# Where the tiles of a two-block transformer kernel start within the 2048-byte rows of SBUF

## The reference, cut to what matters

```python
def swiglu(h, w_gu, w_down):
    g, u = jnp.split(h @ w_gu, 2, axis=-1)          # 1024 -> 2 x 2816
    return (jax.nn.silu(g) * u) @ w_down            # 2816 -> 1024
...
for l in range(DEPTH):                              # first block, DEPTH = 2
    x = x + FFN_RESIDUAL * (1 + mod[2])[:, None, :] * swiglu(h, ffn1_w_gu[l], ffn1_w_down[l])
    x = x + (1 + mod[5])[:, None, :] * hybrid_mixer(...)
    x = x + FFN_RESIDUAL * (1 + mod[8])[:, None, :] * swiglu(h, ffn2_w_gu[l], ffn2_w_down[l])
...
for i in range(DEPTH):                              # second block
    x = x + g1[:, None, :] * mixed                  # even_mixer or odd_mixer
    x = x + g2[:, None, :] * conv_ffn(h, ffn_w_in[i], ffn_conv_w[i], ffn_conv_b[i], ffn_w_out[i])
```

## Time and profile before

| | |
|---|---|
| median of three runs | 3612.19 us |
| the profiled execution's own time | 3611.59 us |
| its span | 3609.8 us |
| PE busy | 3360.8 us, 93% |
| DVE, ACT, POOL busy | 54%, 33%, 28% |
| DMA | 116 GB/s on average |
| mean granted clock of TensorE | 0.952 of full speed |

### The profile page before, as it was taken

How to read it: one execution, slowest core, us unless ns; L and a number is a source line. 1 busy time by engine, 2 the same in 40 slices (tenths; PEclk the granted TensorE clock), 3 DMA queues, 4 the chain that set the end, 5 groups by cost and what they waited for, 6 DMA issues and landing times.

```text
span 3609.8 us, 41457 instructions
## 1 busy us (share of the span) xinstructions
PE 3360.8 (93%) x14717; PEld 2649.8 (73%) x14717; DVE 1946.7 (54%) x2809; ACT 1194.0 (33%) x1790; POOL 1011.5 (28%) x713
## 2 busy tenths in 40 slices
PE   6999979999999999978999998999999988599998
PEld 4888756678878888755688886756788867478886
DVE  6534575565356533666665334346654379864443
ACT  3222233532223222323432223254333243243332
POOL 2815530056184800181064004700730021000000
PEclk7999999999999999989999998979999999799999
DMA  6635552155364633352155334601543333023332
GB/s 206 198 109 153 151 156 66 30 163 168 103 190 132 198 95 95 97 174 66 41 175 150 93 94 146 186 1 53 174 140 96 92 97 84 12 70 99 97 94 83
DMA packets 577054, 417.65 MB, mean 116 GB/s; under 512 B 29979, under 2 KB 537226, under 8 KB 575798
## 3 DMA queue, kind: packets, MB, share of 16 engines
q1 hardware_dynamic: 532434, 283.99, 26.8%
q0 software_dynamic: 34304, 121.64, 11.3%
q10 hardware_dynamic: 10212, 10.68, 1.0%
HBM read 408.89 MB, written 6.06 MB: 115 GB/s over the span
## 4 chain that ended last, share of the span: by engine, by line
PE 78%; DVE 15%; ACT 3%; issue 2%; ACTq 0%; DMA 0%; DVEq 0%; SPq 0%
PE bank L313 23%; PE bank L314 23%; PE bank L315 23%; PE bank L1213 2%; PE bank L1244 2%; DVE w_lo L290 1%; DVE tmp L427 1%; PE bank L545 1%; PE bank L1234 1%; DVE w_lo L299 1%; DVE h_lo L437 1%; DVE s_x L2280 1%; DVE s_t L2271 1%; DVE folded L487 1%; DVE s_x L2277 1%
## 5 line engine op out<-in xcount | busy, mean ns | idle before, releaser
L313 PE MATMUL bank<-h_hi,w_hi 128*128 128x512 f32 x2656 | 1055.5, 397 | 74.9 <-DVE w_lo L290 35.9
L314 PE MATMUL bank<-h_lo,w_hi 128*128 128x512 f32 x2656 | 1047.0, 394 | 0.0
L315 PE MATMUL bank<-h_hi,w_lo 128*128 128x512 f32 x2656 | 1045.7, 394 | 0.0
L299 DVE TENSOR_TENSOR w_lo<-raw,w_hi 128x1024 fp32r<-128x1024 f32 x438 | 624.4, 1426 | 594.6 <-ACT w_hi L282 593.7
L282 ACT ACTIVATE w_hi<-raw 128x1024 fp32r<-128x1024 f32 x438 | 461.8, 1054 | 718.7 <-PE bank L315 718.6
L313 PEld LDWEIGHTS bank<-h_hi,w_hi 128*128 128x128 f32 x2656 | 505.7, 190 | 200.5 <-issue 48.9
L315 PEld LDWEIGHTS bank<-h_hi,w_lo 128*128 128x128 f32 x2656 | 505.3, 190 | 109.0
L314 PEld LDWEIGHTS bank<-h_lo,w_hi 128*128 128x128 f32 x2656 | 505.9, 190 | 105.5 <-issue 0.2
L624 POOL TENSOR_TENSOR mod_acc<-mod_acc,mod_w 128x1024 f32<-128x1024 f32 x168 | 473.1, 2816 | 14.0
L313 PE MATMUL bank<-hid_hi,w_hi 128*128 128x512 f32 x1056 | 421.5, 399 | 13.9 <-DVE w_lo L299 13.6
L314 PE MATMUL bank<-hid_lo,w_hi 128*128 128x512 f32 x1056 | 419.2, 397 | 0.0
(11 more groups left out here) (314 smaller groups left out, 3465.6 us busy)
## 6 DMA issues: line engine op xcount, KB each, us to landing
raw<-in_ffn_w_gu SPq DMA_DIRECT2D x176, 512.0 KB, 3.8
mod_w<-in_w_ada POOLq DMA_DIRECT2D x128, 512.0 KB, 4.1
mod_w<-in_mod_w POOLq DMA_DIRECT2D x96, 512.0 KB, 4.2
raw<-in_ffn_w_in SPq DMA_DIRECT2D x88, 512.0 KB, 3.8
raw<-in_ffn_w_down SPq DMA_DIRECT2D x64, 512.0 KB, 4.1
raw<-in_w_in SPq DMA_DIRECT2D x34, 512.0 KB, 4.0
raw<-in_ffn_w_out SPq DMA_DIRECT2D x32, 512.0 KB, 4.1
raw<-in_ffn_w_down SPq DMA_DIRECT2D x32, 384.0 KB, 3.5
```

Of the source, the lines that this page charges most:

```text
L299: loop(nc.vector.tensor_tensor(w_lo[:, u % 2, :], raw[:, u % 2, :], w_hi[:, u % 2, :].bitcast(F32), ALU.subtract), "split_lo", times)
L313: nc.tensor.matmul(dst, a_hi, b_hi, start=start, stop=False)
L314: nc.tensor.matmul(dst, a_hi, b_lo, start=False, stop=False)
L315: return nc.tensor.matmul(dst, a_lo, b_hi, start=False, stop=stop)
```

## The change

Four things are done to the placement, and nothing else. The small tiles that are not streamed in 512 columns (`cols`, `ident`, `ones`, `cact`, `stat`, `eps`, `misc`, `shape_col`, `inv_rms`, `folded_col`) come first, from byte 16512 on. The cursor is then rounded up to the next multiple of 2048, 22528, and the tiles from `x` to `sq` follow. `group` becomes 129024, which is 63 x 2048. Four tiles (`folded`, `swap`, `coef`, `smx`) go to a strip above the last multiple of 2048 in the usable bytes. No instruction is added, removed or reordered.

```diff
+ROW = 4 * S
...
+        top = nc.sbuf_usable_end // ROW * ROW
+        tail = [top]
...
-            assert where[0] <= nc.sbuf_usable_end, (name, where[0])
+            assert where[0] <= (nc.sbuf_usable_end if where is tail else top), (name, where[0])
...
+        cols = place("cols", [P, ROW_TILES * P])
+        ident = place("ident", [P, P])
+        ones = place("ones", [P, P])
+        cact = place("cact", [P, 2 * KT])
+        stat = place("stat", [P, 32])
+        eps = place("eps", [P, 1])
+        misc = place("misc", [P, 8])
+        shape_col = place("shape_col", [P, 4])
+        inv_rms = place("inv_rms", [P, S])
+        folded_col = place("folded_col", [P, 2])
+        cursor[0] = (cursor[0] + ROW - 1) // ROW * ROW
         x = place("x", [P, KT, S])
...
-        cols = place("cols", [P, ROW_TILES * P])
...
-        folded_col = place("folded_col", [P, 2])
         group = cursor[0]
+        folded = place("folded", [P, 2, P], F32, tail)
+        swap = place("swap", [P, P], F32, tail)
+        coef = place("coef", [P, 2, 24], F32, tail)
+        smx = place("smx", [P, 48], F32, tail)
```

More of the change, by code:

```diff
@@ L171, in emit @@
         cursor = [(nc.sbuf_base + 63) // 64 * 64]
-        names = {}
+        top = nc.sbuf_usable_end // ROW * ROW
+        tail = [top]
         def place(name, shape, dt=F32, where=cursor):
```

## The result

The changed kernel takes 3586.59 us (median of four runs, 3580.33 to 3589.54), against 3613.27 us for the kernel before in the same comparison. The ratio is 0.9927, with a 95% interval of 0.9908 to 0.9947. So the change is faster by 0.7%, where 4% was forecast. The forecast failed; one of its rivals (only the relation counts, 3588 us) came out to within 2 us. The profiled execution has a span of 3586.5 us, 23.3 us less than before.

What follows compares the result with a forecast made beforehand. TensorE's back-to-back float32r matmul steps were taken to bound the kernel: 3611.6 - 156.4 (shorter steps) + 10 (lost in waits) = 3465 us, forecast as 3466 since that execution lies 0.6 below the median; range 3434 to 3490.

Steps and rivals of the forecast that it cites:

- only the relation counts: Rival: stream's place relative to weights mod 512 matters; h stays 226.9 ns, hid joins it; 3588 us, chance 0.16.
- The step that failed: In h and hid streams, excess of 13.4 and 20.0 ns a step was tied to 2048-byte boundary cuts.
- The step that is left: For streamed matmuls after the change: 216.0 ns, from 213.3 of clocks plus 2.7 seen in 128-column passes.
- relation, or nothing: Sign that the forecast is wrong: h steps still at 226.6 ns after the change.
- the boundary law: Streamed reads: excess equals the shorter part cut by a 2048-byte boundary, 128 bytes for h, 192 for hid.
- The sum: TensorE gains of 87.3 (h-like), 66.7 (shared region) and 2.4 us (lat), together 156.4, less 10 lost in waits.
- half of it: Rival: boundary is one part of the excess, a relation the other; step near 221 ns, about 3535 us, chance 0.07.
- What doesn't come back: Where TensorE waits for a unit's w_lo, set by VectorE, saved time is lost again: 10 us.
- The small tiles: Moved tiles read by ScalarE and VectorE: nothing taken, either sign open, about 7 us either way.
- Slower: Rival: weights and stream starting at the same place of a 2048-byte row collide; 51 us more, 3663 us, chance 0.06.
- Placement does nothing: Rival: the excess is what a float32r step costs, h and hid differ for other reasons; 3612 us, chance 0.09.

Runs made afterwards that it cites:

- the sweep: Kernel without the computation: groups of 40 back-to-back matmuls, each with one placement of weights and stream; float32r steps 226.7 to 227.3 ns at distance 0.
- everything at 1856: Kernel before, four small tiles moved in front of x, so x to sq and the shared region start 1856 past a multiple of 2048: 3590.22 us, ratio 0.9931.
- one tile moved: Kernel before, with coef (192 bytes) moved behind the shared region, which then starts 1664 past a multiple of 2048: 3587.36 us, ratio 0.9916.
- distance 256: Kernel before, with three small tiles (448 bytes) moved behind the shared region, which then starts 1408 past a multiple of 2048: 3588.84 us, ratio 0.9922.
- the weights 64 bytes off: Kernel before, with cact (64 bytes) moved between h_lo and raw, so the weights start at 192 while x and h stay at 128: 3656.83 us, ratio 1.0124.
- L63: Group of back-to-back matmuls using 32 partitions, in a kernel without the computation, against a base group at 226.5 ns a step; ran partly at the lower clock.

## Why the prediction was wrong

**The step that failed** is the reading of two numbers as a law: "So the excess of both is the shorter of the two parts in which a 2048-byte boundary cuts the 512 columns", with "both give zero at a multiple of 2048". 32 and 48 clocks fitted 128 bytes and 192 bytes exactly. But the excess takes few values here (the sweep has 32 clocks at distance 0, 37.5 at 192 and 41 to 50 at all others but 240, which has 32 again), so a match of two of them was no strong evidence. The 32 clocks of `h` belonged to distance 0, not to an offset of 128, and the 48 of `hid` to weights at 128 beside a stream at 1856, a distance of 64 (mod 256).

**The evidence against it was in the prediction**: with weights from `lat` the step was 230 at the same stream offset of 128. The step changed while the start of the stream kept its place. That alone says that the stream's own boundary can't be the whole cause, and it deserved more than 0.16. In the earlier trace rows the distance is 320 - 128 = 192, for which the sweep has 229.0 (228.9 for the very pair). The 230 of the earlier trace rows was read as an effect of the weights' start as well, and that isn't shown: those weights have 32 columns, and the sweep has 231.6 for 32 columns at distance 0 and 230.7 at 128, the two distances that the earlier trace rows alternate. So the width alone is enough for it.

**The step that is left**, forecast at 216.0, is 226.9 for `h`, the prediction's own sign for "relation, or nothing". The nearest row was taken from passes of 128 columns at two clocks a column, which don't read at full rate. The prediction said so and used them all the same; the ground for it was the boundary law, by which nothing but such a small rest should remain. The Trainium skill (page "TensorE: Matmul & The Clock Gate", section "Wait — 56ns, not 53.3ns?") gives N / 2.4 GHz plus about 2.5 ns. The sweep agrees for bfloat16 (215.8), finds the same 2.5 ns over the 1024 clocks of a float32 pass (429.2), and disagrees for float32r (226.7 at best).

**The sum**, with measured terms: 8011 x 0 for the `h`-like steps instead of 87.3 us; 3853 x 6.5 = 25.0 us for the shared region instead of 66.7; `lat` 149 x 0.9 = 0.1 instead of 2.4. Together 25.1 us, against 23.3 us of span and 26.7 between the medians. One of the prediction's other sums is off: by its own counts a step of 221 (the rival "half of it") gives 96 us and takes 10 back, 3526 us and not 3535.

**What doesn't come back** was right in kind: the phases in which TensorE waits for `w_lo` got shorter by 2.1 and 2.3 us (134.84 to 132.78, 135.90 to 133.59), the four others by 3.5 each. That is 2.7 us given back, where the rival allowed 2 and the forecast, for a larger gain, 10. Some 0.4 of it are steps at the lower clock, which never had the excess.

**The small tiles** were costed at nothing. VectorE is busy 13 us less over the run and ScalarE 0.9 us more, the splits at line 299 (302 after) have their old mean (1426 ns before, 1433 after), and three other placements of these tiles (everything at 1856, one tile moved, distance 256) come to 3587 to 3590 us. Nothing of the time is theirs within what can be measured, some 7 us.

**The rivals.** "Only the relation counts" was right in its mechanism, its steps and its time. It named a period of 512 bytes, and it is 256. "Slower" was priced at 51 us for a bad relation; the weights 64 bytes off make one, and it cost 43. It couldn't come from this change, since distance 0 is the best place and not a bad one. "Placement does nothing" is refuted by 192 bytes that are worth 0.8%. The page that the prediction named beside it (the Trainium skill, page "SBUF — State Buffer", section "Operand start alignment") says that it is about legality and that its runs timed nothing, so it neither supports nor contradicts this.

## What to carry to other kernels

For float32r matmuls of 128x128 weights with 512 streamed columns, place the weight tiles and the streamed tiles, high and low parts alike, so that their starts agree mod 256 bytes: 226.7 ns a step against 229 to 234 at nearly all other distances. It's enough to move one small tile, and any small tile put between the two can lose it again. The rule isn't for other shapes: 96 weight columns are best at a distance of 128, and 256 streamed columns are slowest at 0. For bfloat16 and plain float32 no unequal starts were run. When one number fits a formula, look in the same trace for a place where the formula's input stays and the number changes, before a forecast is built on it.

## What was not expected

- With 128 weight columns, 512 streamed ones and the same distance in every pass, the step follows a difference of two addresses with a period of 256 bytes, to within about 1 ns, and 4 bytes are enough to move it: 226.7 ns at 0 and 240, 232.4 at 4, 229.0 at 192. Alternating distances don't average.
- A weight operand of fewer columns can be slower: 8 columns have 226.8 ns, 1 and 16 columns 231, 32 columns 231.6, 64 and 96 columns 230.0, all at distance 0.
- With 32 of 128 partitions in use (L63 above), the granted clock fell although matmuls ran back to back. It was seen once, and nothing tests the cause. The first line is the window of the two groups before, the second that of this group (length, busy and count, granted clock):

```profile
57.00:75.00 18.00, 18.00 (x80) 1.00 0.00 0
76.00:89.00 13.00, 13.00 (x39) 0.63 0.01 1
```

With 64 partitions (first sweep) it stayed at full speed: 227.6 ns a step.
